# Fourth and fifth slice of the stream behind four norms, on GpSimd instead of VectorE

## The reference

```python
for i in range(DEPTH):                      # DEPTH = 2
    mix = gated_deltanet(...) if i % 2 == 0 else mlstm(...)   # of rms_norm(hs, norm_w[i, 0])
    hs = hs + keep * rms_norm(mix, norm_w[i, 1])
    f = conv_ffn(rms_norm(hs, norm_w[i, 2]), ...)             # 1024 -> 2 x 2816 -> 1024
    hs = hs + keep * rms_norm(f, norm_w[i, 3])
```

## Time and profile before

| | |
|---|---|
| median of three runs | 1445.06 us |
| span of the profiled execution | 1443.1 us |
| TensorE matmuls busy | 1423.5 us (99%) |
| VectorE busy | 1013.4 us (70%) |
| ScalarE busy | 779.4 us (54%) |
| GpSimd busy | 294.0 us (20%) |
| DMA | 155 GB/s mean |

### The profile page before, as it was taken

The page is one execution under the profiler, slowest core; times in us unless marked ns, Lnnn a source line. Parts: engine busy times, 40 slices in busy tenths (PEclk is TensorE's granted clock), DMA queues, the critical chain, the costliest instruction groups (busy, mean ns, idle before and its releaser), DMA issues.

```text
span 1443.1 us, 31771 instructions
## 1 busy us (share of the span) xinstructions
PE 1423.5 (99%) x11333; PEld 1363.9 (95%) x11333; DVE 1013.4 (70%) x1701; ACT 779.4 (54%) x1399; POOL 294.0 (20%) x348
## 2 busy tenths in 40 slices
PE   9999999999999999999999999999999999999997
PEld 8999888899999999999999999999999989999986
DVE  7884957659876477569888477587664687776645
ACT  6556324556655366466565356464453567654542
POOL 3804002103444000002544000013330012033310
PEclk9999999999999999999999999999999999999999
DMA  7551231244655535344666544546556433565552
GB/s 256 177 175 47 88 101 47 93 142 160 190 175 175 175 119 189 103 146 128 193 189 189 182 134 152 164 146 200 183 168 204 152 116 118 163 217 186 183 180 91
DMA packets 60996, 223.57 MB, mean 155 GB/s; under 512 B 6768, under 2 KB 6896, under 8 KB 60528
## 3 DMA queue, kind: packets, MB, share of 16 engines
q1 hardware_dynamic: 60624, 220.17, 48.1%
q10 hardware_dynamic: 288, 2.23, 0.4%
HBM read 221.32 MB, written 1.05 MB: 154 GB/s over the span
## 4 chain that ended last, share of the span: by engine, by line
PE 81%; DVE 12%; issue 3%; ACT 3%; DVEq 1%; ACTq 0%; POOL 0%; POOLq 0%
PE bank L440 20%; PE bank L441 20%; PE bank L442 20%; DVE wlo L415 3%; PE bank L461 2%; PE bank L1168 2%; PE bank L462 1%; PE bank L468 1%; DVE bank L947 1%; PE bank L3284 1%; PE bank L3285 1%; PE bank L3287 1%; ACT cv L831 1%; DVE cv L839 1%; DVE work L1782 1%
## 5 line engine op out<-in xcount | busy, mean ns | idle before, releaser
L415 DVE TENSOR_TENSOR wlo<-raw,whi 128x1024 fp32r<-128x1024 f32 x397 | 501.4, 1268 | 249.3 <-ACT whi L410 248.8
L410 ACT ACTIVATE whi<-raw 128x1024 fp32r<-128x1024 f32 x397 | 415.1, 1056 | 288.6 <-PE bank L442 240.6
L440 PE MATMUL bank<-xs,whi 128*128 128x258 f32 (+2 forms) x1984 | 569.2, 287 | 0.0
L441 PE MATMUL bank<-xs,whi 128*128 128x258 f32 (+2 forms) x1984 | 563.9, 284 | 0.0
L442 PE MATMUL bank<-xs,wlo 128*128 128x258 f32 (+2 forms) x1984 | 561.6, 283 | 0.0
L440 PEld LDWEIGHTS bank<-xs,whi 128*128 128x128 f32 x1984 | 374.2, 189 | 3.0 <-issue 1.6
L442 PEld LDWEIGHTS bank<-xs,wlo 128*128 128x128 f32 x1984 | 375.0, 189 | 0.0
L441 PEld LDWEIGHTS bank<-xs,whi 128*128 128x128 f32 x1984 | 374.3, 189 | 0.6 <-issue 0.2
L440 PE MATMUL bank<-hf,whi 128*128 (+3 forms) x848 | 241.3, 285 | 2.0 <-DVE cv L839 0.8
L441 PE MATMUL bank<-hf,whi 128*128 (+3 forms) x848 | 240.3, 283 | 0.0
L442 PE MATMUL bank<-hf,wlo 128*128 (+3 forms) x848 | 240.2, 283 | 0.0
(11 more groups left out here) (516 smaller groups left out, 1671.8 us busy)
## 6 DMA issues: line engine op xcount, KB each, us to landing
raw<-stream SPq DMA_DIRECT2D x412, 512.0 KB, 3.7
con<-consts SPq DMA_DIRECT2D x1, 1284.5 KB, 10.5
big<-mla ACTq DMA_DIRECT2D x1, 1152.0 KB, 7.8
hs_sb<-hs SPq DMA_DIRECT2D x2, 544.0 KB, 4.2
work<-last ACTq DMA_DIRECT2D x1, 1024.0 KB, 9.1
y_out<-work SPq DMA_DIRECT2D x4, 256.0 KB, 2.0
par<-params SPq DMA_DIRECT2D x1, 420.0 KB, 7.9
par<-params SPq DMA_DIRECT2D x1, 224.0 KB, 4.8
```

What stands on the lines that cost most here:

```text
L410: nc.scalar.activation(whi[:, s, :], raw[:, s, :], ACT.Copy).then_inc(hi_split, 1)
L415: nc.vector.tensor_tensor(wlo[:, s, :], raw[:, s, :], whi[:, s, :].bitcast(F32), ALU.subtract).then_inc(block_split, 1)
L440: nc.tensor.matmul(out_, whi[:, slot, w], hi, start=start, stop=False)
L441: nc.tensor.matmul(out_, whi[:, slot, w], lo, start=False, stop=False)
```

## The change

GpSimd gets a function `add_pool` that does multiplication and addition of slices 3 and 4 for each of the four norms, ahead of its next work in its list. VectorE's `add_y` returns at once for these two slices. ScalarE's high parts wait for the addition of whichever engine does it. GpSimd waits for the scale and for VectorE's weighted copy of the slice out of PSUM.

```diff
+    POOLED = (3, 4)
+
+    def add_pool(pool, name):
+        pl, t = S("norm", "pool"), slice(POST_FIRST[name], T1)
+        pool.wait_ge(*S("norm", "act").at(f"{name}_scale"))
+        for m in POOLED:
+            pool.wait_ge(bank_free, G[name] + m + 1)
+            nc.gpsimd.tensor_tensor(y[:, m, t], y[:, m, t], rs[:, 1, t], ALU.mult).then_inc(*pl.mark(f"{name}_y{m}"))
+            pool.wait_ge(*pl.at(f"{name}_y{m}"))
+            nc.gpsimd.tensor_tensor(hs[:, m, t], hs[:, m, t], y[:, m, t], ALU.add).then_inc(*pl.mark(f"{name}_h{m}"))
+
+    added = lambda name, m: S("norm", "pool" if m in POOLED else "dve").at(f"{name}_h{m}")
+
     def add_y(dve, name, m):
+        if m in POOLED:
+            return
...
         for m in range(KC):                      # next_act, and the same in last_act
-            act.wait_ge(*S("norm", "dve").at(f"{post}_h{m}"))
+            act.wait_ge(*added(post, m))
...
         gdn_pool(pool)
+        add_pool(pool, "post0")
         ffn_pool(pool, 0, G["up0"])
+        add_pool(pool, "post1")
         ml_pool(pool)
+        add_pool(pool, "post2")
         ffn_pool(pool, 1, G["up1"])
+        add_pool(pool, "post3")
         ffn_pool(pool, 2, G["up2"])
```

## The result

The changed kernel takes **1453.21 us** (median of 4 runs, 1452.6 to 1457.46) against 1445.05 (4 runs, 1444.93 to 1445.1): a ratio of 1.0057, 95% interval 1.0046 to 1.0069, slower by 8.2 us. The prediction was 1449.1 with a range of 1445.8 to 1450.8: the sign is right, the size is half, and the time lies outside the range. The profiled execution of the changed kernel has a span of 1455.6 us, 12.5 more than that of before.

What follows compares the result with a forecast made beforehand. TensorE holds 81% of the chain, with VectorE pacing the wave behind each norm. Turns less recovery, +0.97, +0.97, +0.83 and +1.21 us, sum to +4.0 on the 1445.06 median: 1449.1 us, range 1445.8 to 1450.8.

Steps and rivals of the forecast that it cites:

- The turns: Behind each norm's weight split, VectorE and GpSimd alternate instructions, 0.62 and 0.28 us per turn at 272 columns.
- Addition 2: VectorE's addition of slice 2, releasing hi 2 and its matmuls: 1.95 us late at 272 columns, 1.89 at other widths.
- the order: Behind the weight split: y3, y0, h3, h0, y4, y1, h4, h1, with 3 and 4 on GpSimd.
- Hi 3 and hi 4: ScalarE's high parts of slices 3 and 4: GpSimd's additions done before hi 2, so TensorE never waits for them.
- The first rival: No exclusion between short VectorE and GpSimd instructions: all 3.7 us won, 1441.4 us; chance 0.11.
- the second rival: VectorE keeps the port while its next instruction is issued: addition 2 1.27 late, 0.3 net per norm, 1446.3 us; chance 0.16.
- the third: Turns of whole instructions: 3.15 and 3.01 us late, net 8.6 us, 1453.7 us; chance 0.06.
- The recovery: VectorE, relieved of slices 3 and 4, stops pacing the wave: 0.98, 0.98, 1.06 and 0.68 us back per norm.
- own time: TensorE from its first matmul on hi 2 to tile 3: 7.2, 7.2, 6.87 and 6.81 us predicted.
- the forecast's own range: Whole change slower by 3.0 to 5.3 us, 1448.0 to 1450.4, before widening for rivals; forecast's chance 0.67.

Runs made afterwards that it cites:

- only the relief: Kernel before, VectorE's multiplications and additions of slices 3 and 4 left out and done by nobody: 1441.4 us, ratio 0.9964.
- its repeat: The changed kernel run once more, unedited, for the spread of its times and a second trace: 1455.37 us, ratio 1.0055.
- the four products: Kernel before, VectorE doing all its work, plus four GpSimd products per norm on unread columns: 1455.45 us, ratio 1.0061.
- the gaps filled: Changed kernel with spare TensorE matmuls: 26, 5 and 3 per wave 1452.52 us; 27, 8 and 4 1451.51 us; these plus twelve at 116 us 1450.71 us.
- before with spare matmuls in the waves: Kernel before with spare TensorE matmuls, 26 instead of 16 ahead of the wave, 5 and 3 behind slices 0 and 1: 1448.49 us, ratio 1.0018.
- the twelve at 116 us: Kernel before with twelve spare 128-column matmuls in TensorE's gap in the first mixer: 1445.73 us, ratio 0.9996.
- with memsets: Kernel before with four write-only GpSimd memsets of 816 unread columns behind each norm's scale: 1445.72 us, ratio 1.0.
- one slice later: Changed kernel with only slice 4 on GpSimd, starting when VectorE's addition 2 is done: 1449.29 us, ratio 1.0018.
- one slice at once: Changed kernel with only slice 4 on GpSimd, same release: 1449.91 us, ratio 1.0025.
- before without the 16 products: Kernel before without TensorE's 16 unused products between the sum of squares and the wave: 1449.05 us, ratio 1.0017.
- the run that had none: Profiled run of the changed kernel with 26, 5 and 3 spare matmuls per wave: 1449.74 us, span 1448.0.
- the last run above: Changed kernel with 27, 8 and 4 spare matmuls in the waves and twelve at 116 us: 1450.71 us, ratio 1.0029.

## Why the prediction was wrong

**The turns: right.** Addition 2 was to be 1.95 and 1.89 us late; it is 1.97, 2.03, 1.93 and 1.89. In three norms of the first profile even the order was the predicted one, GpSimd first; in the first norm, VectorE's multiplication 0 slipped in ahead (319.34, 0.43 us) and a low part paid instead. Hi 3 and hi 4 never waited for GpSimd. The first rival (no exclusion) needed 0.43 us beside GpSimd and is out for products and additions, though it holds for memsets; the second needed additions 1.27 late; the third's time, 1453.7, is close to the measured one, but turns of whole instructions would have made addition 2 late by 3.15 us. A right time would have come from a wrong cause.

**The recovery: the step that failed.** "So the whole 0.98 comes back, and next late is TensorE itself", 0.98, 0.98, 1.06 and 0.68 us per norm, took 0.124 us per matmul from stretches without gaps. As a limit of the wave it was right: 7.26 us where only the relief is there, where spare matmuls fill the gaps, and 6.82 in the one wave of the changed kernel that kept its clock. What was missing is what the step of turns does to TensorE: it spreads 15 matmuls over 3.7 us (321.31 to 325.03) behind waits of 1.19 and 0.82, and the granted clock goes to 0.50 for 3.4 or 6.8 us. In the profiled run the own time was 8.05, 7.86, 8.47 and 7.90, so it gave back 0.11, 0.30, -0.55 and -0.41 us: a sum of -0.55 and not 3.70. A second sentence failed with it, "Addition 2 and with it hi 2 and its matmuls follow unchanged and are as late": the clock is already down for half or more of the matmuls on slice 1, and hi 2's first matmul comes 0.75, 1.43, 1.50 and 0.90 us behind addition 2 instead of some 0.6, another 2.2 us. The 7.8 us of the turns, these 2.2 and the 0.55 are the 10.6 by which tile 3 is late.

**How firmly the cause is shown.** In the profiles of kernels with four turns and no spare matmuls (the changed one, its repeat, the four products) 10 of 12 waves fell. Eight of the 12 begin with a gap of 1.6 to 1.8 us and a second of 0.65 to 0.82: all eight fell. In the other four VectorE's multiplication 0 went ahead of GpSimd's and the first gap is 1.1 to 1.2 us: two fell (the first norm in both profiles of the changed kernel), two held (the first norm with the four products, the fourth in the repeat). With four turns and the gaps filled (what is left of them is under 0.7 us), 0 of 12 fell. With TensorE's gaps at the start of the wave as before, or filled (the kernel before; before with spare matmuls in the waves, with the twelve at 116 us, with memsets, with only the relief; one slice later) 0 of 24. In between lie one slice at once, 1 of 4, and before without the 16 products, 2 of 4; both have one long gap and a short one or none behind it. So the gaps bring the falls on: one long gap in 3 of these 8 waves, two gaps one behind the other in 10 of 12. Which waves fall, and for 3.4 or 6.8 us, differs between executions of one kernel, and the spread from 1450.3 to 1457.5 goes with the mean clock, 0.998 to 0.991. Why the same gaps (1.19 and 0.82 us in the first norm) let the clock fall in two profiles and not in a third stays open.

**The sum, redone.** Without falls the change costs 4.9 us by the span of the run that had none, 4.7 to 5.2 by the best runs, against a forecast of 4.0: the forecast's own range of 3.0 to 5.3 holds it. About 0.7 of the 4.9 is the spare matmuls' own, by an estimate: in the third and fourth norm of that run the first matmul on hi 2 comes 0.94 and 0.89 us behind addition 2, and in the kernel before 0.60 and 0.55. No run without spare matmuls shows these waves at full clock with GpSimd first. With VectorE first, the fourth wave is 1.18 late without them and 1.24 with them (the last run above). The turns are 2.01 + 2.01 + 1.96 + 1.91 = 7.9 there instead of 7.7; less the predicted 3.7 that makes the 4.2 that are left. The falls in the waves then add about 10.6 - 4.2 = 6.4 us in the profiled run. The fall at 119 us puts the first norm off by 1.4 to 2.6 us in the eight traces that have it. It isn't the change's, for 26 of the kernel before's 65 later runs lie in the upper group too; but it lasts 6.8 us in the four traces with `add_pool` and 3.4 in the four without, and why stays open. The median of the four runs, 8.2 us above before, has 3 to 4 us of falls; how much of it lies in the waves no trace shows, since the profiled run is the slowest of the four. In the prediction, the second rival's 0.3 us per norm comes to 1.4 us in all and not 1.2 (0.29 + 0.29 + 0.21 + 0.59), which changes nothing.

The Trainium skill ("SBUF — State Buffer", section "SBUF: two separate sides") was weighed in the prediction as a lock that the loser waits out in full. The runs here show an exclusion, and a smaller one than that: a GpSimd product cost VectorE 0.45 to 0.58 us, not 0.77.

## What to carry to other kernels

Moving a two-operand instruction from VectorE to GpSimd beside a busy VectorE spares VectorE 0.43 us and costs it about 0.5 (at 272 columns): look for a time when VectorE waits, or leave it. When a change delays the first pieces of a pipelined stream, add a term for the consumer's clock: here waits of about 1 us between short groups of matmuls put what followed at half the clock, and a rate read from a gap-free stretch no longer holds. Where one kernel's runs spread by several us, list the granted clock per stretch before explaining a difference; spare matmuls in the gaps tell whether it is the clock, over several runs and with the clock read where it matters, for one kernel with them gave 1449.74 and 1454.4 us.

## What the runs showed of the hardware

- GpSimd's products and additions in SBUF and VectorE's alternate instruction by instruction, 0.89 to 0.99 us per VectorE instruction instead of 0.43 to 0.50; GpSimd's memsets of 816 columns (0.8 us each) leave VectorE at 0.43 to 0.44.
- TensorE's granted clock went to 0.50 behind a first gap of 1.1 to 1.8 us, or behind that and a second of 0.65 to 0.82, around groups of six and nine matmuls, for 3.41 or 6.83 us, in which TensorE was busy but for the second gap where the fall began ahead of it. Behind a first gap of 1.6 to 1.8 us and a second of 0.65 to 0.82 it fell in 8 of 8 waves, behind a first of 1.1 to 1.2 in 2 of 4.
- The kernel before has two values, 1444.9 to 1446.0 and 1447.0 to 1448.1 us, some 2.5 apart, at mean clocks of 0.998 to 0.999 and 0.997. With twelve spare matmuls ahead of 119 us, where eight of the fourteen profiles show a fall, the upper value was gone in 11 runs.
